# Stage 1's state products in three bf16 passes, and stage 2's keys by token turned instead of computed

## The reference

```python
# first block, 4 heads, dk 128, dv 256, chunks of 64
a_intra = jnp.einsum('bhnid,bhnjd->bhnij', q * jnp.exp(b - mid), k * jnp.exp(mid - b))
a_intra = jnp.where(causal, a_intra, 0.0)
o = jnp.einsum('bhnij,bhnje->bhnie', a_intra, v)
kv = jnp.einsum('bhnjd,bhnje->bhnde', k * jnp.exp(b_last - b), v)
def step(state, inp):
    dec, kv_n = inp
    return dec[..., None] * state + kv_n, state
...
o = o + jnp.einsum('bhnid,nbhde->bhnie', q * jnp.exp(b), states)
...
o = rmsnorm(o, norm_g)
o = o.reshape(B, S, GLA_DV).astype(h.dtype) * jax.nn.silu(r)
return o @ w_out
# second block, mLSTM branch, 4 heads of 96
k = jnp.einsum('bshd,hde->bhse', ch, wk).astype(f32)
...
s = jnp.einsum('bhtd,bhsd->bhts', qb, kb) * jnp.exp(dmat - m_t[..., None])
C_next = carry_scale[..., None, None] * C + jnp.einsum('bhs,bhse,bhsd->bhed', ws, vb, kb)
```

## Time and profile before

| | |
|---|---|
| time, median of 3 runs | 2473.06 us (2468.83 to 2474.91) |
| the profiled execution's own time | 2479.82 us |
| its span, first to last instruction | 2478.0 us |
| mean granted TensorE clock | 0.953 |
| TensorE busy (matmul) | 2200.6 us, 89% |
| VectorE, ScalarE, GpSimd busy | 61%, 42%, 23% |

### The profile page before, as it was taken

The page is one execution under the profiler, slowest core; times in us unless marked ns, Lnnn a source line. Parts: engine busy times, 40 slices in busy tenths (PEclk is TensorE's granted clock), DMA queues, the critical chain, the costliest instruction groups (busy, mean ns, idle before and its releaser), DMA issues. The chain is left out here.

```text
span 2478.0 us, 49033 instructions
## 1 busy us (share of the span) xinstructions
PE 2200.6 (89%) x20402; PEld 1566.2 (63%) x20402; DVE 1518.6 (61%) x2358; ACT 1050.5 (42%) x2294; POOL 569.1 (23%) x538
## 2 busy tenths in 40 slices
PE   2799999999999981599999999999996499898988
PEld 1476666666666641498998898999985144343333
DVE  6644334444444434666767665666664797988885
ACT  2334333433333421423333332233332497887774
POOL 0510000000000103133234333332333132323321
PEclk9999999999999995799999999999997699999999
DMA  9300000000000006301001000010001803011111
GB/s 399 118 18 19 18 27 18 19 27 18 19 26 19 27 9 253 128 26 30 25 25 36 28 25 28 25 31 25 25 27 35 284 1 94 27 61 60 60 52 51
DMA packets 82332, 139.03 MB, mean 56 GB/s; under 512 B 42432, under 2 KB 63040, under 8 KB 78016
## 3 DMA queue, kind: packets, MB, share of 16 engines
q1 hardware_dynamic: 82112, 135.79, 15.6%
HBM read 104.30 MB, written 31.46 MB: 55 GB/s over the span
## 5 line engine op out<-in xcount | busy, mean ns | idle before, releaser
L1311 PE MATMUL m_bank<-m_arena,m_w_hi 128*128 128x128 bf16 (+1 forms) x2560 | 444.5, 222 | 22.5 <-DVE m_w_lo L1283 22.1
L1312 PE MATMUL m_bank<-m_arena,m_w_hi 128*128 128x128 bf16 (+1 forms) x2560 | 444.0, 219 | 0.0
L1313 PE MATMUL m_bank<-m_arena,m_w_lo 128*128 128x128 bf16 (+1 forms) x2560 | 443.8, 219 | 0.0
L1311 PEld LDWEIGHTS m_bank<-m_arena,m_w_hi 128*128 128x128 bf16 (+1 forms) x2560 | 249.4, 97 | 28.4 <-DVE m_w_lo L1283 22.5
L1312 PEld LDWEIGHTS m_bank<-m_arena,m_w_hi 128*128 128x128 bf16 (+1 forms) x2560 | 254.1, 99 | 0.3
L1313 PEld LDWEIGHTS m_bank<-m_arena,m_w_lo 128*128 128x128 bf16 (+1 forms) x2560 | 248.0, 97 | 0.0
L1688 POOL TENSOR_TENSOR s_hi<-s_sp,s_cols 128x512 bf16<-128x512 f32 x144 | 152.3, 1057 | 366.8 <-DVE s_sp L1819 156.4
L218 POOL TENSOR_TENSOR g_stage<-g_stage,g_nh_row 128x1024 f32<-128x1024 f32 x16 | 52.3, 3269 | 734.9 <-DVE g_stage L487 734.9
L553 PE MATMUL g_bank<-g_wi_hi,g_h_hi 128*128 128x512 bf16 x512 | 194.2, 379 | 0.7 <-ACT g_stage L290 0.7
L554 PE MATMUL g_bank<-g_wi_lo,g_h_hi 128*128 128x512 bf16 x512 | 194.0, 379 | 0.0
L555 PE MATMUL g_bank<-g_wi_hi,g_h_lo 128*128 128x512 bf16 x512 | 194.0, 379 | 0.0
(11 more groups left out here) (361 smaller groups left out, 5653.2 us busy)
## 6 DMA issues: line engine op xcount, KB each, us to landing
m_arena<-in_w_in_dram SPq DMA_DIRECT2D x8, 1618.0 KB, 8.6
g_stage<-in_gla_w_in_dram SPq DMA_DIRECT2D x8, 1552.0 KB, 12.5
g_stage<-in_ada_w_dram SPq DMA_DIRECT2D x8, 1536.0 KB, 11.2
g_xs<-in_x_dram SPq DMA_DIRECT2D x16, 512.0 KB, 3.5
x<-g_stage SPq DMA_DIRECT2D x16, 512.0 KB, 2.7
m_arena<-in_w_mod_dram SPq DMA_DIRECT2D x8, 1024.0 KB, 6.9
m_arena<-x SPq DMA_DIRECT2D x16, 512.0 KB, 3.5
s_xr<-x SPq DMA_DIRECT2D x16, 512.0 KB, 4.0
```

Source lines behind the costliest of these rows:

```text
L1311: pe.matmul(out, l_hi, r_hi, start=(k == 0), stop=False)
L1312: pe.matmul(out, l_hi, r_lo, start=False, stop=False)
L1313: ins = pe.matmul(out, l_lo, r_hi, start=False, stop=(k == n - 1))
```

## The change

Stage 1. The three groups of f32 products become three bf16 passes each. Their operands are split into halves: v (high half on ScalarE as it leaves the bank, low half on VectorE: `v_lower`), the turned keys (high on ScalarE, low on VectorE), the scaled queries e_b and the masked scores (high on ScalarE, low on GpSimd: new function `low`), and the state, which is updated in place and split at the tile's end (high on ScalarE, low on GpSimd, 1024 columns).

Stage 2. The product of k by token goes; the copied k by feature (`kT`) is turned by four transposes into the same bank B5, after sq and sk, and the first half of `turn_x` moves ahead of the key-value product.

```diff
@@ gla_phase, GpSimd
+            def low(out, name, hi_name, src, hi, i):
+                pool.wait_ge(s[hi_name], i + 1)
+                pool.tensor_tensor(out, src, hi, ALU.subtract).then_inc(s[name], 1)
+
             def tile(i):
 
+                low(eb_hl[:, 1, :], "eb_lo", "eb_hi", e_b, eb_hl[:, 0, :], i)
+                low(am_hl[:, 1, :], "am_lo", "am_hi", am, am_hl[:, 0, :], i)
                 pool.wait_ge(s["silu_arg"], i + 1)
...
+                low(st_hl[:, 1], "st_lo", "st_hi", st, st_hl[:, 0], i)
@@ ScalarE
-                    act.activation(v_sb[:, n * 512:(n + 1) * 512], bank[:], ACT.Copy).then_inc(s["v_copied"], 1)
+                    act.activation(v_hl[:, 0, n * 512:(n + 1) * 512], bank[:], ACT.Copy).then_inc(s["v_copied"], 1)
...
+                act.wait_ge(s["eb_scaled"], i + 1)
+                act.activation(eb_hl[:, 0, :], e_b, ACT.Copy).then_inc(s["eb_hi"], 1)
                 act.wait_ge(s["kl_turned"], i + 1)
-                act.activation(klT, TR[:], ACT.Copy).then_inc(s["klT_copied"], 1)
+                act.activation(kl_hl[:, 0, :], TR[:], ACT.Copy).then_inc(s["klT_copied"], 1)
+                act.wait_ge(s["am_done"], i + 1)
+                act.activation(am_hl[:, 0, :], am, ACT.Copy).then_inc(s["am_hi"], 1)
...
                 act.activation(sg, sg, ACT.Exp).then_inc(s["silu_exp"], 1)
+                act.wait_ge(s["state_done"], i + 1)
+                act.activation(st_hl[:, 0], st, ACT.Copy).then_inc(s["st_hi"], 1)
@@ VectorE
+            def v_lower(i, n):
+                dve.wait_ge(s["v_copied"], 2 * i + n + 1)
+                half = slice(n * 512, (n + 1) * 512)
+                dve.tensor_tensor(v_hl[:, 1, half], (G0, G1)[n][:], v_hl[:, 0, half], ALU.subtract).then_inc(s["v_low"], 1)
...
+                v_lower(i, 0)
                 if not first:
                     y_add(i - 1, 1 - par, link)
                 if not last:
                     x_norm(i + 1, 1 - par)
+                v_lower(i, 1)
...
                 dve.copy_predicated(am, causal[:], A[:]).then_inc(s["am_done"], 1)
+                dve.wait_ge(s["klT_copied"], i + 1)
+                dve.tensor_tensor(kl_hl[:, 1, :], TR[:], kl_hl[:, 0, :], ALU.subtract).then_inc(s["kl_low"], 1)
...
-                old, new = st[par], st[1 - par]
+                wait("st_lo", i)
                 for h in range(GH):
-                    ins = dve.scalar_tensor_tensor(new[:, h, :], old[:, h, :], dec_t[:, h:h + 1],
+                    ins = dve.scalar_tensor_tensor(st[:, h, :], st[:, h, :], dec_t[:, h:h + 1],
@@ TensorE (turn_x waits for kl_low in place of klT_copied, the r products for v_low in place of v_copied)
-                pe.wait_ge(s["klT_copied"], i + 1)
+                TERMS = ((0, 0), (0, 1), (1, 0))
...
+                pe.wait_ge(s["kl_low"], i + 1)
                 wait("state_done", i)
                 for h in range(GH):
-                    ins = pe.matmul(KV[h // 2][:, (h % 2) * GDV:(h % 2 + 1) * GDV], klT[:, h * GDK:(h + 1) * GDK],
-                                    v_sb[:, h * GDV:(h + 1) * GDV], start=True, stop=True)
+                    for n, (l, r) in enumerate(TERMS):
+                        ins = pe.matmul(KV[h // 2][:, part(h)], kl_hl[:, l, h * GDK:(h + 1) * GDK],
+                                        v_hl[:, r, h * GDV:(h + 1) * GDV], start=(n == 0), stop=(n == 2))
                 ins.then_inc(s["kv_done"], 1)
                 wait("og_done", i)
-                pe.wait_ge(s["eb_scaled"], i + 1)
+                wait("st_lo", i)
+                pe.wait_ge(s["eb_lo"], i + 1)
...
@@ mix_phase
-                dve.wait_ge(s["qk_done"], i + 1)
+                dve.wait_ge(s["ktok_turned"], i + 1)
                 dve.tensor_copy(k_tok, B5[:, 0:MW].rearrange("p (h e) -> p h e", h=MH)).then_inc(s["ktok_copied"], 1)
...
-                    pe.matmul(B4[0:MD, hs], wk_sb[:, n, :], cu[:, b, :], start=first_b, stop=last_b)
-                    ins = pe.matmul(B5[:, h * MD:(h + 1) * MD], cu[:, b, :], wk_sb[:, n, :],
-                                    start=first_b, stop=last_b)
+                    ins = pe.matmul(B4[0:MD, hs], wk_sb[:, n, :], cu[:, b, :], start=first_b, stop=last_b)
...
                 pe.wait_ge(s["qk_copied"], i + 1)
+                wait("pT_copied", 3 * i)
+                for h in range(MH):
+                    ins = pe.transpose(B5[:, h * MD:(h + 1) * MD], kT[0:MD, h, :], ident[0:MD, 0:MD])
+                ins.then_inc(s["ktok_turned"], 1)
                 wait("oa_done", i)
...
+                if not last:
+                    turn_x(i + 1, 0)
                 pe.wait_ge(s["ktok_copied"], i + 1)
                 pe.wait_ge(s["vw_done"], i + 1)
...
                 if not last:
-                    turn_x(i + 1)
+                    turn_x(i + 1, 1)
```

More of the change, by code:

```diff
@@ L94, in gla_phase @@
         am = carve(512)
-        st = [carve3(GH, GDV) for _ in range(NC)]
+        st = carve3(GH, GDV)
+        st_hl = carve(D).bitcast(BF16).rearrange("p (v h e) -> p v h e", v=2, h=GH)
         og_hi = carve(512).bitcast(BF16)
@@ L532, in _ @@
             pre.done(dve.memset(am, 0.0))
-            pre.done(dve.memset(st[0], 0.0))
+            pre.done(dve.memset(st, 0.0))
+            pre.done(dve.memset(st_hl, 0.0))
             tile(0, 0, first=True)
@@ L580, in turn_x @@
                     if n == 0:
-                        wait("klT_copied", i)
+                        wait("kl_low", i)
                     else:
@@ L662, in tile, with part @@
                     turn_x(i + 1)
[L663 removed]
+                TERMS = ((0, 0), (0, 1), (1, 0))
+                def part(h):
+                    return slice(h % 2 * GDV, (h % 2 + 1) * GDV)
+                pe.wait_ge(s["kl_low"], i + 1)
                 wait("state_done", i)
                 for h in range(GH):
[L666 to L667 removed]
+                    for n, (l, r) in enumerate(TERMS):
+                        ins = pe.matmul(KV[h // 2][:, part(h)], kl_hl[:, l, h * GDK:(h + 1) * GDK],
+                                        v_hl[:, r, h * GDV:(h + 1) * GDV], start=(n == 0), stop=(n == 2))
                 ins.then_inc(s["kv_done"], 1)
                 wait("og_done", i)
[L670 removed]
+                wait("st_lo", i)
+                pe.wait_ge(s["eb_lo"], i + 1)
                 for h in range(GH):
[L672 to L674 removed]
+                    for n, (l, r) in enumerate(TERMS):
+                        pe.matmul(O[h // 2][:, part(h)], eb_hl[:, l, h * T:(h + 1) * T], st_hl[:, r, h, :],
+                                  start=(n == 0 and h % 2 == 0), stop=False, skip_group_check=True)
+                pe.wait_ge(s["am_lo"], i + 1)
                 for h in range(GH):
[L676 to L677 removed]
+                    for l, r in TERMS:
+                        ins = pe.matmul(O[h // 2][:, part(h)], am_hl[:, l, h * T:(h + 1) * T],
+                                        v_hl[:, r, h * GDV:(h + 1) * GDV], start=False, stop=True, skip_group_check=True)
                 ins.then_inc(s["o_done"], 1)
@@ L1336, in _, with turn_x @@
             pe.wait_ge(s["mod_out"], 1)
-            def turn_x(i):
+            def turn_x(i, n):
                 pe.wait_ge(s["xn_done"], i + 1)
-                for n, bank in enumerate((TR, B5)):
-                    if n == 0:
-                        wait("ya_done", i - 1)
-                        wait("cols_exp", i)
-                    else:
-                        wait("ktok_copied", i)
-                    for m in range(4):
-                        kb = 4 * n + m
-                        ins = pe.transpose(bank[:, m * T:(m + 1) * T], xn[:, kb * P:(kb + 1) * P], ident[:])
-                    ins.then_inc(s["xT_done"], 1)
+                if n == 0:
+                    wait("ya_done", i - 1)
+                    wait("cols_exp", i)
+                else:
+                    wait("ktok_copied", i)
+                for m in range(4):
+                    kb = 4 * n + m
+                    ins = pe.transpose((TR, B5)[n][:, m * T:(m + 1) * T], xn[:, kb * P:(kb + 1) * P], ident[:])
+                ins.then_inc(s["xT_done"], 1)
             def turn_p(i, first):
@@ L1479, in tile @@
                 ins.then_inc(s["scores_done"], 1)
-            turn_x(0)
+            turn_x(0, 0)
+            turn_x(0, 1)
             pe.wait_ge(s["w_lo"], KB)
```

17 lines of the change are left out of this document (7 added, 10 removed).

## The result

The changed kernel takes 2491.41 us in the median of 7 runs (2476.98 to 2497.98), the kernel before 2473.21 (2468.83 to 2479.27, 7 runs): ratio 1.006, 95% interval 1.0033 to 1.0088. It is slower by more than the 0.3% that can be told apart, and lies outside the range of 2461 to 2483.

A forecast was written before the change was run, and what follows sets the result against it. TensorE's work was taken to bound both stages. Stage 1 +6.0 us (first tile +9.4, loop -3.0, last tile -0.4) and stage 2 -8.0 sum to -2.0; forecast 2473 us, range 2461 to 2483.

The forecast's parts named there:

- The bound and TensorE's work: Both stages: TensorE's work bounds them; in stage 1, 36 bf16 products take 3.96 us for 5.19, 1.23 less a tile.
- The new wait for the h chain: Stage 1 loop tiles: TensorE newly waits about 0.9 us a tile for VectorE's L392, leaving 5.0 us gained.
- L518 blocked by the state's low half: Stage 1 loop: GpSimd's low half (2.3 us) holds the port lock, so VectorE's L493, now L518, ends some 2.2 us later.
- What is late next: `y_products` need L399.: Stage 1 loop: y_products have slack 1.95 us, exceeded by 0.25 us in eight tiles, so 2.0 us are lost.
- Rival 2: Stage 1 loop: state's low half takes 3.3 us, not 2.3, delaying L493; loop +10.3 us, 2486 us, chance 0.14.
- The first tile: Stage 1's first tile: TensorE waits 8.9 us for GpSimd, still splitting w_out, then runs at low clock: +9.4 us.
- The last tile: Stage 1's last tile: no h chain, output hangs on the key-value product, a third of the 1.23 us gained: -0.4 us.
- Stage 2: Transposes at 0.45 us save 0.75 us a tile; tiles 53.02 or 54.68 us, a low-clock spell in every tile: -8.0 us.
- rival 1: Stage 2: low-clock spells stay as frequent as now, -12.0 us there; 2467 us, chance 0.24.
- Rivals 1, 3 and 4: Besides rival 1, stage 1: 3, full 1.23 us counts, 2459 us, chance 0.06; 4, no first-tile wait, 2464 us, 0.06.

The follow-up runs named there:

- e10: Changed kernel with state's low half late, TensorE's loop written out, first tile's low halves on VectorE, h chain early, stage 2's window products later: 2426.28 us, ratio 0.9810.
- e13: Changed kernel with the state's low half made in the next tile and TensorE's stage 1 loop written out: 2469.40 us, ratio 0.9971.
- e7: Kernel before with TensorE's stage 1 loop written out, so no jump back: 2469.74 us, ratio 0.9991 to the kernel before.
- e3: Changed stage 1 with the kernel before's stage 2, state's low half made in the next tile: 2488.07 us, ratio 1.0061 to the kernel before.
- e4: Changed stage 1 with the kernel before's stage 2, TensorE's stage 1 loop written out: 2493.08 us, ratio 1.0078 to the kernel before.
- e2: Kernel before with only stage 2 changed: 2461.64 us, ratio 0.9958 to the kernel before.
- e9: Kernel before with stage 2 changed and its window products and turn_h moved behind the tv product: 2450.45 us, ratio 0.9907 to the kernel before.
- e11: Kernel before with TensorE's stage 1 loop written out and stage 2's window products moved behind the tv product: 2456.66 us, ratio 0.9930.

## Why the prediction was wrong

- **The bound and TensorE's work**: right. 36 products in place of 12 save 1.2 to 1.3 us a tile (forecast 1.23): a tile goes from 52.28 to 50.94 net of its waits, or to 51.1 in e10.
- **The new wait for the h chain**: right, 1.01 us a tile (forecast 0.9). Work and wait together give -4.6 us, for -5.0 forecast; without any jump the loop takes 727.31 us (e13) against 731.92 (e7), -4.6 again.
- **L518 blocked by the state's low half**: the mechanism was right, 3.07 us for an operation of 1.23, and e3 took it away. The Trainium skill, "SBUF — State Buffer", section "SBUF: two separate sides", has the exclusive lock for a whole instruction; the trace agrees: L518 started 0.14 us behind GpSimd's 2.13 us and lost 1.84.
- **The step that failed first**: "What is late next: `y_products` need L399." I took the consumer whose wait I had been looking for and computed its slack (1.95 us), and did not follow the other thing that hangs on the blocked product: the gate, behind which ScalarE copies k. Its slack was 0.9. This cost 8.0 us in place of 2.0, and 1.0 more in the last tile. Rival 2 named L493 and nearly the sum (+10.3 for the loop, 2486 us), but by a longer low half, which did not come (2.13 us), and with the wrong point from which it decides; that its sum comes near is luck.
- **The step that was missing**: TensorE's own jump at the loop's end, on the place where the change takes work out. Put at nothing, it cost 8.9 us more than before. The order of the program shows the jump's place, and the gaps of 0.5 to 0.8 us at L555 in the trace of before were its trace. I read neither. e4 and e7 show it from both sides.
- **The first tile**: right, +9.6 for +9.4, by the mechanism named (L706, low clock behind), with two sizes off that cancel. The last tile: +1.4 in place of -0.4. The copy of k costs it 1.0 us, and L518 itself another 1.9: TensorE has nothing else to do there until L522, which follows L518, and waits 9.1 us for it (6.1 before, 7.2 in e3, where the product is short). I had only the gain of the products there.
- **Stage 2**: the two lengths of a tile were right to 0.2 us. The transposes were mis-sized: four of them take 0.33 us from start to start, not 0.45, so that a tile without a spell is 0.88 us shorter (53.77 to 52.89) and not 0.75. At the frequency of spells as it was that would be -14.1 in sixteen tiles, not rival 1's -12.0; the median gives -11.7 (e2), against my -8.0. So part of the gain did go to more spells, but less than I had. And tiles neither all lock to a spell, nor stay free of it: e13 has twelve in a row, the first profile four and then nine without. Within a row of such tiles a spell begins 0.05 to 0.12 us later in each, which may be how the lock is lost in the end.
- **Rivals 1, 3 and 4**: 1 is about right for stage 2 alone, though its 2467 counts from 2473.06 where the others count from my 2473 and its -2.0 (from there it is 2469); 3 and 4 are out.

With the two missed terms (+6.0 and +8.9) and the last tile's 1.8 the sum for stage 1 would have been 22.7 for the 23.06 measured. What stays open: what starts a spell of low clock in stage 2. e9 shows only that it is not the 1.06 us wait.

## What to carry to other kernels

When a change makes one operation late, list everything that stands behind it on every engine, copies that TensorE needs above all, and compute the slack of each; the nearest is not the one that a wait in the old profile points to. And before shortening the work at the end of a loop, look at what it hides there: the sequencer's jump, the next tile's chain. A gain on the critical engine is only had when the two or three waits close behind it are taken away in the same step: here +18 us became -47. Of these, 17 us are what two of the edits (the loop written out, the window products later) give the kernel before as well (e11); against e11 the change is worth 30.

## What the hardware showed beyond that

- TensorE's jump back takes 3.3 to 3.9 us from the branch to the next instruction, with a fetch of 16 KB of instructions in it (0.9 to 1.2 us), and is followed by a second gap, 0.5 to 1.6 us from start to start. That the fetch is what makes the jump long is not shown. Branches of the other four engines at the end of their stage 1 loops take 40 to 67 ns.
- TensorE's sequencer runs ahead by a number of products, not by a time: at the jump 17 f32 records or 16 bf16 ones have still to start, which is 3.5 us of the first and 1.7 us of the second, the same at all seven branches. Making products shorter makes everything that only the queue hid more visible.
- The written-out loop of fourteen tiles showed no gap for fetching instructions above 0.2 us (e4, e7, e10).
- A spell of low clock (3.4 us) costs a tile of stage 2 1.6 to 1.7 us wherever it falls, and tiles near 54.6 us in length fall into step with it, for four to twelve tiles.
